# Merging the two root events of an attention head and shortening the head's schedule in a hand-ordered two-block kernel

## What is computed

```
p = h @ w_in                                  # h: normed and modulated x; for the 256 context rows too
q = rope(rms_norm(q, g0)); k = [rms_norm(kc, g1), rope(rms_norm(k, g1))]     # 4 heads, two maps of 64 columns each
s = q @ k.T * 64 ** -0.5                      # for map 0 and map 1
p = softmax(s0) - lam * softmax(s1)
o = rms_norm(p @ v) * (1 - lam_init)          # v of 128 columns, per head
x = x + gate * (concat(fourier, pool, o) * silu(g)) @ w_out
```

## Time and profile before

| | |
|---|---|
| median of 3 runs | 2099.54 us (2099.49 to 2100.87) |
| profiled execution | 2096.87 us, its span 2095.6 us |
| TensorE busy | 2031.4 us, 97% of the span |
| VectorE busy | 1362.9 us, 65% |
| ScalarE busy | 871.2 us, 42% |
| mean granted TensorE clock | 0.990 |

### The profile page before, as it was taken

One profiled execution on the slowest core, in us unless ns is written; L12 is line 12 of the kernel. 1 busy time (PEld: TensorE's weight loads), 2 busy tenths in 40 slices (PEclk: granted clock), 3 DMA queues, 4 the chain that ended last, 5 costly groups with the idle time before them and its releaser, 6 DMA issues.

```text
span 2095.6 us, 26198 instructions
## 1 busy us (share of the span) xinstructions
PE 2031.4 (97%) x10342; PEld 1696.5 (81%) x10342; DVE 1362.9 (65%) x1953; ACT 871.2 (42%) x1364; POOL 118.5 (6%) x155
## 2 busy tenths in 40 slices
PE   6999999989999989999999999999999999999998
PEld 2888888878888868888888888888888888888886
DVE  6678777667768776854677536657785467644554
ACT  4367766225677433133463223236223354322321
POOL 1000000110000130000000000000000000000000
PEclk9999999999999999999999999999999999999999
DMA  8322222333223356342336435534543234433332
GB/s 306 116 71 71 66 70 67 101 116 101 81 71 91 111 160 188 121 121 71 91 111 181 121 104 157 148 93 134 160 138 92 71 111 136 116 111 101 92 98 82
DMA packets 313273, 238.22 MB, mean 114 GB/s; under 512 B 6976, under 2 KB 289984, under 8 KB 312512
## 3 DMA queue, kind: packets, MB, share of 16 engines
q1 hardware_dynamic: 294000, 166.81, 27.0%
q0 software_dynamic: 18432, 67.12, 10.5%
q10 hardware_dynamic: 720, 2.62, 0.4%
HBM read 234.42 MB, written 2.10 MB: 113 GB/s over the span
## 4 chain that ended last, share of the span: by engine, by line
PE 85%; DVE 5%; ACT 5%; issue 3%; DMA 2%; SPq 0%; POOL 0%; DVEq 0%; ACTq 0%; POOLq 0%
PE ps L621 65%; PE ps L594 4%; PE ps L2600 2%; PE ps L1558 1%; ACT a_p L1825 1%; PE ps L1539 1%; PE ps L1540 1%; PE ps L1569 1%; DMA first_mod<-in_w_mod_first 1%; PE ps L2580 1%; DMA mod_w_out<-in_ada_w_turned 1%; PE ps L1487 1%; PE ps L1436 1%; PE ps L2667 1%; DVE w_lo_second L577 1%
## 5 line engine op out<-in xcount | busy, mean ns | idle before, releaser
L621 PE MATMUL ps<-h_second_hi,w_hi_second 128*128 128x512 f32 x1120 | 448.8, 401 | 1.9 <-ACT w_hi_second L557 1.9
L621 PE MATMUL ps<-h_second_lo,w_hi_second 128*128 128x512 f32 x1120 | 438.2, 391 | 0.0
L621 PE MATMUL ps<-h_second_hi,w_lo_second 128*128 128x512 f32 x1120 | 277.1, 389 | 0.4 <-DVE w_lo_second L577 0.4
L577 DVE TENSOR_TENSOR w_lo_second<-w_raw_second,w_hi_second 128x1024 fp32r<-128x1024 f32 x160 | 196.7, 1230 | 94.8 <-ACT w_hi_second L557 94.8
L621 PEld LDWEIGHTS ps<-h_second_hi,w_hi_second 128*128 128x128 f32 x1120 | 211.7, 189 | 47.5 <-ACT w_hi_second L557 2.7
L621 PEld LDWEIGHTS ps<-h_second_lo,w_hi_second 128*128 128x128 f32 x1120 | 211.6, 189 | 44.1 <-issue 1.9
L621 PEld LDWEIGHTS ps<-h_second_hi,w_lo_second 128*128 128x128 f32 x1120 | 210.1, 188 | 45.3 <-DVE w_lo_second L577 0.8
L621 PE MATMUL ps<-h_hi,w_hi_first 128*128 128x512 f32 (+1 forms) x592 | 205.6, 361 | 5.1 <-DVE proj L1915 2.3
L621 PE MATMUL ps<-h_lo,w_hi_first 128*128 128x512 f32 (+1 forms) x592 | 202.1, 355 | 0.0
L557 ACT ACTIVATE w_hi_second<-w_raw_second 128x1024 fp32r<-128x1024 f32 x168 | 176.1, 1049 | 42.2 <-PE ps L621 33.4
L2986 ACT ACTIVATE conv<-ps,cols 128x512 f32<-128x512 f32 x44 | 34.4, 781 | 252.3 <-PE ps L621 250.0
(11 more groups left out here) (351 smaller groups left out, 3634.2 us busy)
## 6 DMA issues: line engine op xcount, KB each, us to landing
w_raw_second<-in_w_in SPq DMA_DIRECT2D x64, 512.0 KB, 4.6
w_raw_first<-in_w_in SPq DMA_DIRECT2D x48, 512.0 KB, 3.8
mod_w_mixer<-in_ada_w_turned POOLq DMA_DIRECT2D x48, 512.0 KB, 4.0
w_raw_second<-in_w_gate SPq DMA_DIRECT2D x44, 512.0 KB, 4.0
w_raw_second<-in_w_val SPq DMA_DIRECT2D x44, 512.0 KB, 4.7
w_raw_down<-in_w_down SPq DMA_DIRECT2D x32, 704.0 KB, 4.6
mod_w_ffn<-in_ada_w_turned POOLq DMA_DIRECT2D x32, 512.0 KB, 4.0
mod_w_in<-in_w_mod_turned POOLq DMA_DIRECT2D x27, 512.0 KB, 3.8
```

Of the source, the lines that this page charges most:

```text
L577: k.nc.vector.tensor_tensor(lo, raw, hi.bitcast(F32), ALU.subtract).then_inc(k.sem.weight_split_v, 1)
L621: last = tensor.matmul(k.ps[:, bank, 0:count], w[:, q * P:(q + 1) * P], rows[q][:, first:first + count], start=(n == 1), stop=(n == 3 * t.k))
```

## The change

- The sums of key and query of a head are formed together at r=4, both in bank 7 side by side; ScalarE takes both roots there, with a one-element Sqrt ahead of its wait and a one-element Exp behind the roots, each of which makes the table be loaded at that place. VectorE inverts at r=5 and r=7, the key's roots are widened at r=6, spread at r=7 and 9, values turned at r=11 and 13. Two heads can now be in these steps at once (`heads_at`).
- Scores begin at step 35 instead of 31, preparation at 31 instead of 27; a head takes 14 steps in layer 0 and 13 in layer 1 instead of 15 and 14. The order of units in a head stays.
- Head norms: group 0 from step 66, group 1 ends at 91; the sum of the last head in layer 1 is at 93. Their roots load the tables in the same way.
- The lag of the second tile is 1 in layer 0 and 2 in layer 1 instead of 4; the copy of the folded weights moves from step 3 to 5.
- In steps 13 and 17 VectorE splits the weights ahead of the pooling.

```diff
-FIRST_LAGS, SECOND_LAGS = (0, 4), (0, 2, 3)
-HEAD_STEPS, VALUE_LAG = (15, 14), (5, 6)
+FIRST_LAGS, SECOND_LAGS = ((0, 1), (0, 2)), (0, 2, 3)
+HEAD_STEPS, VALUE_LAG = (14, 13), (5, 6)
+HEAD_ROOTS, KEY_SPREADS, VALUE_TURNS = 4, (7, 9), (11, 13)
 def score_step(l, h, j):
-    return 31 + HEAD_STEPS[l] * h + SCORE_STEPS[l][j]
+    return 35 + HEAD_STEPS[l] * h + SCORE_STEPS[l][j]
...
+def heads_at(s):
+    return [(h, s - 21 - 12 * h) for h in range(HEADS) if 0 <= s - 21 - 12 * h < 16]
...
 def rope_tensor(k, l, h, r):
-    if r in (0, 6):
-        j = (0, 6).index(r)
-        tensor.wait_ge(*k.evacuated[own[4 + 3 * h + j]])
-        if j:
-            tensor.wait_ge(n.k_scaled, 2 * at + 2)
-        elif h:
+    if r == HEAD_ROOTS:
+        if h:
             tensor.wait_ge(n.v_copied, 2 * at)
-        for c in range((TA, SPAN[l])[j] // P):
-            last = tensor.matmul(k.ps[:, 7, 2 * c:2 * c + 2], k.head_sq[j][:, c * P:(c + 1) * P], k.ones_half[:, 0:P:QK],
-                                 start=True, stop=True)
+        for j in (0, 1):
+            tensor.wait_ge(*k.evacuated[own[4 + 3 * h + j]])
+            for c in range((TA, SPAN[l])[j] // P):
+                last = tensor.matmul(sums_view(k, j)[:, 2 * c:2 * c + 2], k.head_sq[j][:, c * P:(c + 1) * P],
+                                     k.ones_half[:, 0:P:QK], start=True, stop=True)
         last.then_inc(n.qk_summed, 1)
...
-HEAD_GROUPS = (((0, 1), 64, 68, 71, 74), ((2,), 80, 82, 84, 87))
-LAST_HEAD = ((93, 95), (89, 91))
+HEAD_GROUPS = (((0, 1), 66, 72, 75, 78), ((2,), 80, 86, 88, 91))
+LAST_HEAD = ((93, 95), (89, 93))
...
-        h, r = head_at(s, 27, HEAD_STEPS[l])
+        h, r = head_at(s, 31, HEAD_STEPS[l])
         if h is not None:
             prepare_scalar(k, l, h, r)
...
 def fourier_scalar(k, l, s):
-    if s == 3:
+    if s == 5:
...
+def load_table(k, function):
+    column = 62 if function == ACT.Sqrt else 63
+    k.nc.scalar.activation(k.small[:, column:column + 1], k.eps[:, 0:1], function)
...
 def rope_scalar(k, l, h, r):
+    if r == HEAD_ROOTS:
+        load_table(k, ACT.Sqrt)
+        scalar.wait_ge(n.qk_summed, at + 1)
+        for j in (0, 1):
+            count = 2 * (TA, SPAN[l])[j] // P
+            scalar.activation((k.k_roots, k.q_roots)[j][:, 0:count], sums_view(k, j)[:, 0:count], ACT.Sqrt,
+                              bias=k.eps[:, 0:1], scale=1.0 / QK).then_inc(n.qk_rooted, 1)
+        load_table(k, ACT.Exp)
+    if r == HEAD_ROOTS + 2:
         scalar.wait_ge(n.qk_inverted, 2 * at + 1)
...
 def first_vector(k, l):
+        if s in (13, 17):
+            split_tile_vector(k, own[i + 1])
         if s in (13, 17, 19, 20):
             pool_vector(k, l, (13, 17, 19, 20).index(s))
```

More of the change, by code:

```diff
@@ L1377, in first_tensor @@
 def first_tensor(k, l, ready):
-    multiply_staggered(k, k.stage_tiles["in", l][0], FIRST_LAGS, ready)
+    multiply_staggered(k, k.stage_tiles["in", l][0], FIRST_LAGS[l], ready)
     if l:
@@ L1405, in first_products @@
     attention_tensor(k, l, s)
-    h, r = head_at(s, 21, 12)
-    if h is not None:
+    for h, r in heads_at(s):
         rope_tensor(k, l, h, r)
@@ L1498, in rope_tensor @@
         last.then_inc(n.k_spread, 1)
-    if r in (8, 10):
-        j = (8, 10).index(r)
+    if r in VALUE_TURNS:
+        j = VALUE_TURNS.index(r)
         tensor.wait_ge(*k.evacuated[own[6 + 3 * h]])
@@ L1504, in rope_tensor @@
         else:
-            tensor.wait_ge(n.qk_rooted, 2 * at + 2)
+            tensor.wait_ge(n.k_scaled, 2 * at + 2)
         for c in range((4, 2)[j]):
@@ L1508, in rope_tensor, with sums_view @@
         last.then_inc(n.v_turned, 1)
+def sums_view(k, j):
+    return k.ps[:, 7, 12 * j:12 * j + 12]
 def keys_of(j):
@@ L1856, in root_first_heads @@
     scalar.activation(roots, roots, ACT.Sqrt).then_inc(n.head_rooted, 1)
+    if g < 2:
+        load_table(k, ACT.Exp)
 def roots_of_group(k, g):
@@ L1897, in first_vector @@
             maxima_vector(k, l, h, j)
-        if s % 4 == 1 and i + 1 < len(own):
+        if s % 4 == 1 and i + 1 < len(own) and s not in (13, 17):
             split_tile_vector(k, own[i + 1])
@@ L1976, in rope_vector @@
         vector.tensor_tensor(place, place, sines, ALU.add).then_inc(n.qk_roped, 1)
-    if r in (3, 5):
-        j = (3, 5).index(r)
+    if r in KEY_SPREADS:
+        j = KEY_SPREADS.index(r)
         first, count = LENGTHS[0][j]
```

19 lines of the change are left out of this document (6 added, 13 removed).

## The result

The changed kernel takes 2107.63 us (median of 6 runs, 2106.21 to 2111.05), the kernel before 2100.20 beside it: a ratio of 1.0036, 95% interval 1.0026 to 1.0046, so it is slower by 7.4 us. Forecast were 2108.7 us and, on the profiled execution, +9.2; its own profiled execution took 2106.21 us with a span of 2104.9, which is +9.3.

What follows compares the result with a forecast made beforehand. TensorE was taken to bound the kernel, busy 222.4 of 231.5 us in layer 0's attention. Terms -3.2 -1.3 -3.7 +16.1 +1.3 +0 = +9.2 us, set on the median, gave 2108.7 us; range 2094 to 2119.

Steps and rivals of the forecast that it cites:

- Part 3, layer 0: Layer 0 head changes: preparation one step too early stalls both queues, a_pt waits; +16.1 us (bounds +5 and +20).
- +16.1 - 3.7: Layer 0: +16.1 us from waits at head changes, -3.7 from score waits behind table loads going.
- Part 3, layer 1: Layer 1 head changes: last score's combination queued behind preparation, waits of 1.7, 3.0, 3.2; net +1.3 us (-4 to +4).
- the spreading waits: Layer 1: key spreading waits for widened roots that stand behind an exponential, 1.7 and 0.4 us.
- -1.3 and +1.3: Layer 1: -1.3 us for the wait at the f_cw copy going, +1.3 for the new head changes.
- Part 2: Joined root event per head: layer 0 score waits for exponentials behind a table load go, -3.7 us (bounds 0 and -3.7).
- Part 1: First two tiles: shorter lag fills TensorE gaps, -3.2 us in layer 0, 0 in layer 1; splits ahead of pooling cost nothing.
- the wait for f_cw: Layer 1: moving the f_cw copy behind tile 0's evacuation removes a wait, -1.3 us (bounds 0 and -1.4).
- The clock: 1.2 GHz stretches in the attention stages, 1.6 us each: taken as 0 (bounds -3.2 and +6.4).
- A: Rival: head changes cost what they cost now and only gains remain; -9.8 us, 2089.7; chance 0.17.
- B: Rival: order counts but waits are half as long (10.7 instead of 21.4 in layer 0); -1.5 us, 2098.0; chance 0.10.
- D: Rival: long waits also lower the clock, layer 1 waits rise to their bound; +18.3 us, 2117.8; chance 0.15.

Runs made afterwards that it cites:

- e2: Kernel before, with only layer 0's head preparation (a_khi, a_klo, a_q, a_qlo) one step earlier on ScalarE and VectorE: 2106.12 us, ratio 1.0037.
- e3: Changed kernel, with VectorE taking the score maxima ahead of the next head's preparation in each step: 2094.69 us, ratio 0.9984.
- e4: As e3, and in layer 0 both halves of a head's preparation stand in the step of the previous head's last score: 2092.07 us, ratio 0.9969.
- e8: Changed kernel, with a head's key sums of squares on TensorE one step ahead of its query sums instead of joined: 2105.43 us, ratio 1.0027.
- e7: As e4, without the one-element operations that call for a table load: 2096.07 us, ratio 0.9988.
- e6: From e4, only orders changed: rotations, layer 1 second preparation half, widened roots, first head group's root, head 0 preparation: 2076.77 us, ratio 0.9895.
- e9: As e6, with a head's key sums on TensorE one step ahead of its query sums instead of joined: 2071.04 us, ratio 0.9858.
- e1: Kernel before, with only the new lags of the first two tiles and the f_cw copy at step 5, no moved splits: 2098.52 us, ratio 0.9998.

## Why the prediction was right, and where not

**Part 3, layer 0: right in mechanism and place.** Waits for a_pt twice at each change of head, with the maxima behind L2028 and the exponential waiting for attention_stats, as forecast; e2 brings such waits into the kernel before, e3 and e4 take them out of after. Their parts against the forecast: 1.60 and 3.53 (1.75 and 3.9), 1.26 and 1.50 (1.4 and 4.9), 0.89 and 6.28 (1.1 and 7.2). The sum is 15.1, against 20.3 and 1.1 for two small ones that did not come. When each second a_pt is ready was good to 0.6 us (T+13.4, T+15.3, T+15.5 against 13.6, 15.5, 16.1). The mis-sized term is when TensorE wants it: for the change 1 to 2 I had it at T+10.6, and it came at T+13.8. The sums stand ahead of it, and there are 24 small matmuls of 2.7 to 2.9 us in the trace, where I counted half; a slow stretch of 3.4 us at 252.7 cost 1.7 more. e8 takes both away, and the wait is 4.41, close to the 4.9 of the forecast. For the stage as a whole my terms (+16.1 - 3.7) gave +12.4 us of idle time and the trace has +6.2: the mechanism came at half its size.

**Part 3, layer 1:** the a_p waits are 2.62, 3.22 and 2.47 (the forecast: 1.7, 3.0, 3.2) and the spreading waits 1.62 (1.7). The second spreading wait (0.4) did not come, and a fourth for a_p, 1.61, did. Idle time in the stage grew by 0.9 us, where -1.3 and +1.3 gave nothing.

**Part 2: the waits went, their price is not shown.** No score waits for an exponential behind a load in layer 0. That this was worth the 3.7 us of my term is not borne out: in e7 score waits of 2.1 us came back and idle time in layer 0 stayed as it was, and the 4.0 us of that pair are waits in layer 1 and clock. What I did not see is the price of the other half: joining the sums is part of the edit, and e6 against e9 puts it at 5.7 us by the medians and 4.9 in the traces, more than my term.

**Part 1: the term right, its cover wrong.** -3.2 became -2.95, and the wait for f_cw went. The first two tiles end at 65.08 (forecast 64.8):

```profile
50.77 14.31 PE ps L594 x78
```

But I wrote that the splits ahead of the pooling cost nothing and gave them no worth, because no row showed TensorE waiting for pool_mean. That was the wrong row to look at: who is late next is the split behind the pooling, not what the pooling makes. In the kernel before it ends at 488.5, and TensorE, 4.1 us later than in e1, came at about 489.4. The slack was 0.9 us, a gain of 4.1 used it up, and e1 is worth nothing.

**The clock: wrong.** I took 0, with bounds of -3.2 and +6.4. In the windows above the same matmuls took 2.85 and 2.1 us longer, so some +5, inside the bounds. I had looked for it behind long waits only; half of it came with the joined sums (e8). It happened to be offset by the waits that were shorter than forecast (15.1 instead of 21.4 in layer 0). That +9.2 stands against +9.3 is luck: two terms were off by 5 to 6 us each, in opposite directions. The direction, and that a loss of some size comes from the changes of head, is not luck.

**The rivals.** A did not come, for the reason given: ScalarE was busy for only 183 of 312.8 us in layer 0, and still could not use the 4.55 us ahead of one exponential for what stood behind it. Nor did B, since the six waits are seven tenths and not half of the forecast. Of D the clock half came for the most part (5.0 of 6.4 us), the layer 1 half did not. A's condition, the maxima within some 5 us of the last score, is nearly met by e3 (6.1, 4.8 and 5.5 us, 2094.7 us) and met by e4 (1.0 to 1.5 us, 2092.1 us), against A's 2089.7.

Open stays why the low level follows some of the joined sums and not others. The second part of the change was not tried alone on the kernel before; what is known of its gain comes from e7 and of its price from e6 and e9, all on kernels with the new heads.

## What to carry to other kernels

When a step is moved in a queue that runs in order, list what stands behind it that someone else waits for; here two changes of order (e3, e4), without any work taken away, were worth 14 us by the ratios and 15.5 by the medians. When a start is brought forward, look for the producer that does not move with it, and compare its end with the consumer's new time: here the slack was 0.9 us, and a gain of 4.1 was lost on it. A forecast wants the same care for when the consumer comes as for when the data are ready, since what is added to the consumer's path ahead of a wait costs nothing.

## What the hardware showed that was not expected

Short runs of very small matmuls, with no idle time, were followed by stretches of TensorE at the lower clock level. In e6, 24 of 2 columns (20 in layer 1), 2.3 to 2.7 us without a gap, were followed within 1 us by the 1.2 GHz level in four of eight cases; the same ones in halves of 1.4 us (e9) in none. In the kernel before, halves were followed by it twice in sixteen, both times with an idle wait of 1.3 to 1.5 us right ahead of them. The second block has such a piece in every kernel, 24 matmuls of one column (in the kernel before from 983.6 to 986.3, the low level from 986.2), and in six of the twelve profiles the low level begins in it or within 1 us of its end. The other thing in or behind which it fell was idle time: 3.10 us in e1, 1.86 in e9, 4.41 in e8. The stretches of 3.4 us cost 1.6 to 1.7 us each when TensorE had work, and nothing where it would have waited anyway.

A sum over two columns of float32 data stands as two records in the trace, 12 products as 24 matmuls at 114 ns from start to start. Whoever counts them by the source counts half.
